# Splitting a convolution's gating by channel halves and moving the rotary products from VectorE to GpSimd

## The chip, the cores and the metric

The kernel runs on one core of a Trainium2 chip. The time is the device time of one launch in microseconds: 1805.58 us before the change, the median of three runs (1804.87 to 1806.22).

## What is computed

A decoder trunk of two layers over 256 tokens of width 1024, all in float32. Each layer has a token mixer with four branches that read one input projection, and a channel mixer (a dense SwiGLU in layer 0, eight experts in layer 1). The change touches two branches:

```
h = rms_norm(x); u = h @ w_in                 # split by columns
# C: convolution module, 512 channels
a, gt = split(u_conv); y = a * sigmoid(gt)
y = causal_depthwise_conv(y, dw, width 31) + db
y_c = silu(layer_norm(y))
# B: attention with an indexer
q, k   = rope_partial(q), rope_partial(k)     # 8 + 2 heads of 64, 16 dims rotated
qi, ki = rope_partial(qi), rope_partial(ki)   # 8 + 1 heads of 32, 8 dims rotated
rope_partial: [x1*cos - x2*sin, x2*cos + x1*sin, rest]
```

The other two branches are a pooling mixer and a state-space scan. The four are gated, summed, projected and added to x.

## The kernel before

**Weights.** All weights come in panels of 128 partitions x 2048 columns, by two DMAs each on SP's queue. A float32 product is done in three passes over a high and a low part: ScalarE copies a panel to `hi_ring` (L538), VectorE writes the remainder raw - hi to `lo_ring` (L1472), and TensorE multiplies (L964, 48 matmuls of 256 columns to a full panel). Both rings have three slots, so ScalarE can copy panel p only when TensorE is done with panel p-3. In the mixer a chunk is one or two panels and ends in a PSUM tile, `pair0` or `pair1` in turn, which ScalarE or VectorE evicts before the next chunk but one may begin. Chunks come in a fixed order: `a` (the values of the convolution), `gt` (its gates), `kwdt`, `kvqi`, `q`, `pool`, `xbc0`, `xbc1`, `z`, `g2h0` and so on.

**Order.** Each engine's program is written out by hand and synchronised by counting semaphores. On VectorE `lo_upto(n)` issues the splits up to panel n, and stands between the other work of the mixer. ScalarE's `evac` (L599) evicts a chunk.

**Convolution.** Tensor `arena` holds the values at A_P and the gates behind them. When both chunks are evicted VectorE multiplies them (L1545, 1024 columns) into a padded tile. The convolution is 31 taps x 4 channel groups of 128: the first tap is L1554, the rest are scalar_tensor_tensor instructions of 256 columns (L1557), all on VectorE, four accumulation chains in turn, with one split after every nine. TensorE then sums the channels for the layer norm (L1069).

**Rotary step.** `swap_pairs` on GpSimd's queue waits until the product has read A_P (`conved` at 1) and until q and then the indexer's keys are evicted, and copies the rotated halves, exchanged, into A_P by 6 + 12 small DMAs (L452). VectorE then does r*sin, v*cos and their sum for the indexer (3 x 256 columns) and for queries and keys (5 x 256): L1574, L1575, L1576, six instructions a layer. TensorE waits for `roped` before it swaps the keys (L1083). Later VectorE uses A_P as scratch for the pooling mixer. In layer 1 the expert stage copies a column of places on GpSimd (L485, L493) ahead of indirect DMAs.

Of the kernel before, what the change touches and what calls it, by code (L numbers as in the profile page):

```python
# [13 lines left out]

# [7 lines left out]
T = 256  # L22
# [3 lines left out]
MG = MIX // 128  # L26
# [3 lines left out]
CONV_W = 31  # L30
# [32 lines left out]
CHUNKS = [("a", 2, "A"), ("gt", 2, "A"), ("kwdt", 1, "A"), ("kvqi", 2, "A"), ("q", 2, "A"), ("pool", 2, "A"),  # L63
# [53 lines left out]
def build(nc, x_d, gains_d, consts_d, params_d, w_in, w_br, w_out, fg, fu, fd, mg, mu, md, out_d, rows_d, sum_d, cums_d):  # L117
# [3 lines left out]
    with ctx:  # L121
# [46 lines left out]
        def raw(slot):  # L168
            if slot < MRING:
# [17 lines left out]
                 "masked", "glued", "conved", "ln_summed", "centred", "ln_squared", "ln_varied", "ln_rooted",  # L187
# [75 lines left out]
        def _(sp):  # L263
# [11 lines left out]
            def mixer(L):  # L275
# [29 lines left out]
                for c0, width in ((C_A, 512), (C_GT, 512), (C_KIWI, KWDT), (C_KVQI, 512), (C_Q, 512), (C_POOL, 512),  # L305
                                  (C_XBC0, 512), (C_XBC1, 256), (C_Z, 512)):
                    if c0 == C_KIWI:
                        narrow()
                    else:
                        chunk_in(c0, width)  # L310
# [129 lines left out]
        def _(pool):  # L440
            pool.dma_start(consts[:, 0:128], consts_d[:, 0:128]).then_inc(ident_in, 16)

            def swap_pairs(L):
                pool.wait_ge(S["conved"], 4 * CONV_W * L + 1)
                pool.wait_ge(*ev(L, "q"))
                for dim, o, p, n in ((64, A_QK, A_P + 3 * T, 5 * T), (32, A_IDX, A_P, 3 * T)):
# [3 lines left out]
                    for a in range(0, 128, dim):  # L450
                        for to, fro, rows in ((a, a + half, half), (a + half, a, half), (a + 2 * half, a + 2 * half, dim - 2 * half)):
                            pool.dma_start(arena[to:to + rows, p:p + n], arena[fro:fro + rows, o:o + n]).then_inc(swapped, 16)  # L452

# [8 lines left out]
            for n in range(5):  # L462
# [7 lines left out]
                if n in (1, 3):  # L470
                    swap_pairs(n // 2)
                    spread_sums(n // 2)
# [52 lines left out]
        def _(act):  # L525
# [56 lines left out]
            def mixer(L):  # L582
# [31 lines left out]
                after("a")  # L614
                evac(ar(A_P, 1024), pair_of("a")[:, :], last=True)
                after("gt")
                evac(ar(A_P + 1024, 1024), pair_of("gt")[:, :], ACT.Sigmoid, last=True)
# [339 lines left out]
        def _(pe):  # L957
# [37 lines left out]
            def mixer(L):  # L995
# [20 lines left out]
                def t_panel(name, kh, groups=4, width=512):  # L1016
# [3 lines left out]
                    if name == "a":  # L1020
# [12 lines left out]
                t_chunk("a")  # L1033
                t_chunk("gt")
# [426 lines left out]
        def _(dve):  # L1461
# [51 lines left out]
            def mixer(L, add_dense=None):  # L1513
# [28 lines left out]
                lo_upto(6)  # L1542

                dve.wait_ge(*ev(L, "gt"))
                link(nc.vector.tensor_tensor(ypad[:, :, CPAD:], ar3(A_P, 4, T), ar3(A_P + 1024, 4, T), ALU.mult))  # L1545
                c0 = 4 * CONV_W * L
                mi = lambda o, n=16: ar(A_MISC + o, n)
                for t in range(CONV_W):
                    for g in range(MG):
                        i = t * MG + g  # L1550
                        src = ypad[:, g, t:t + T]
                        dst = ar(A_CACC + g * T, T)
                        if t == 0:
# [5 lines left out]
                        if i == 100:  # L1559
                            dve.wait_ge(S["ki_copied"], L + 1)  # L1560
                            link(nc.vector.tensor_tensor(ar3(A_MISC + 16, 2, 8), ar3(A_MISC + 16, 2, 8),
                                                         W("dt_bias", 0, 8).unsqueeze(1).broadcast_to([128, 2, 8]), ALU.add))
                            nc.vector.scalar_tensor_tensor(mi(48), mi(16), -1.0, mi(16), ALU.mult, ALU.max)\
                              .then_inc(S["dt_abs"], 1)
                        if i == 116:
                            dve.wait_ge(S["dt_exp"], L + 1)
                            nc.vector.tensor_scalar(mi(64), mi(48), 1.0, None, ALU.add).then_inc(S["dt_plus"], 1)
# [36 lines left out]
                if L == 0:  # L1604
                    dve.wait_ge(const_in, 16)
# [15 lines left out]
                s1, s2 = ar3(A_P, 4, PPAD + T), ar3(A_P + 4 * (PPAD + T), 4, PPAD + T)  # L1621
                link(nc.vector.memset(ar(A_P, 8 * (PPAD + T)).rearrange("p (g t) -> p g t", t=PPAD + T)[:, :, 0:PPAD], 0.0))
# [610 lines left out]
```

## Time and profile before

| | |
|---|---|
| median of 3 runs | 1805.58 us |
| profiled execution | 1806.82 us, span 1805.0 us, mean granted clock 0.992 |
| PE, DVE, ACT, POOL busy | 97%, 82%, 63%, 5% of the span |
| PE in the chain that ended last | 75% |
| DVE in it | 21% |

Times in the rows are microseconds from the start of the span. PE is TensorE, DVE VectorE, ACT ScalarE, POOL GpSimd; L964 is line 964 of the kernel. The chain is followed back from the last instruction, at each step to what released it. A busy time of PE says that matmuls were under way, not that it ran at its peak. The mixer of layer 0 takes about the first 315 us, that of layer 1 begins near 500 us, with the same order of work 497.4 us later.

### The profile page before, as it was taken

To read this page: it belongs to the slowest core of one execution; us is meant where nothing else is said; L and a number is where in the kernel's file an instruction comes from. 1 tells how busy PE (TensorE), PEld (TensorE's weight loads), DVE (VectorE), ACT (ScalarE), POOL (GpSimd) and SP (SyncE) were. 2 spreads that over 40 slices of the span, in tenths; PEclk is the share of its full clock that TensorE was granted. 3 is DMA by queue.
4 is the path that set the end of the run, shared out by engine and by line. 5 is a ranking of instruction groups with operands and counts; after the bars stand their busy time and mean duration, and the time that the engine had idled before them with its cause. 6 is when DMAs were issued, how large, how long until landed. Compare 5 with 4: busy or idle time off the path is not lost.

```text
span 1805.0 us, 27468 instructions
## 1 busy us (share of the span) xinstructions
PE 1752.9 (97%) x10329; PEld 1535.4 (85%) x10329; DVE 1485.7 (82%) x1483; ACT 1144.2 (63%) x976; POOL 84.4 (5%) x101
## 2 busy tenths in 40 slices
PE   7999999999999999999999999999999999999997
PEld 6988888999989988887888888888888888888886
DVE  4998976544459989768979889888898898988987
ACT  4356664444353566646757777777777777777775
POOL 0200000000002000000010000000000000000000
PEclk9999999999999999999999999999999999999999
DMA  8554545755345545448989999999999999999994
GB/s 273 165 163 150 168 150 173 245 187 185 117 153 166 166 142 165 162 173 308 365 320 364 402 365 386 391 375 387 376 365 399 366 387 385 368 397 370 376 407 158
DMA packets 239922, 501.68 MB, mean 278 GB/s; under 512 B 20512, under 2 KB 45104, under 8 KB 239712
## 3 DMA queue, kind: packets, MB, share of 16 engines
q1 hardware_dynamic: 233552, 480.18, 73.9%
q0 software_dynamic: 6288, 20.38, 3.8%
q8 instruction: 55, 0.90, 0.2%
q14 instruction: 27, 0.22, 0.0%
HBM read 490.52 MB, written 7.88 MB: 276 GB/s over the span
## 4 chain that ended last, share of the span: by engine, by line
PE 75%; DVE 21%; ACT 2%; issue 1%; DMA 0%; SPq 0%; DVEq 0%; ACTq 0%
PE pair L964 51%; PE aux L964 20%; DVE lo_ring L1472 7%; DVE arena L1557 5%; PE pair L1387 1%; ACT hi_ring L538 1%; DVE arena L1697 1%; DVE arena L1683 1%; DVE small L1696 1%; DMA raw_ring<-in_w_in 0%; DVE arena L1657 0%; PE aux L1364 0%; DVE act_lo L1647 0%; PE aux L1357 0%; DVE arena L1628 0%
## 5 line engine op out<-in xcount | busy, mean ns | idle before, releaser
L1472 DVE TENSOR_TENSOR lo_ring<-raw_ring,hi_ring 128x2048 fp32r<-128x2048 f32 x276 | 623.5, 2262 | 129.0 <-ACT hi_ring L538 127.1
L538 ACT ACTIVATE hi_ring<-raw_ring 128x2048 fp32r<-128x2048 f32 x276 | 522.4, 1894 | 250.0 <-PE pair L964 170.3
L1472 DVE TENSOR_TENSOR lo_ring<-arena,hi_ring 128x2048 fp32r<-128x2048 f32 x183 | 418.3, 2289 | 75.6 <-ACT hi_ring L538 75.6
L538 ACT ACTIVATE hi_ring<-arena 128x2048 fp32r<-128x2048 f32 x183 | 350.4, 1919 | 138.3 <-PE pair L964 73.0
L964 PE MATMUL pair<-hT_lo,hi_ring 128*128 128x256 f32 (+1 forms) x1360 | 389.9, 287 | 12.9 <-DVE lo_ring L1472 7.0
L964 PE MATMUL pair<-hT_hi,lo_ring 128*128 128x256 f32 (+1 forms) x1360 | 385.8, 284 | 0.0
L964 PE MATMUL pair<-hT_hi,hi_ring 128*128 128x256 f32 (+1 forms) x1360 | 385.7, 284 | 0.0
L964 PE MATMUL pair<-lo_ring,hT_hi 128*128 128x512 f32 x896 | 354.5, 396 | 0.1
L964 PE MATMUL pair<-hi_ring,hT_hi 128*128 128x512 f32 x896 | 349.6, 390 | 0.0
L964 PE MATMUL pair<-hi_ring,hT_lo 128*128 128x512 f32 x896 | 348.8, 389 | 0.0
L964 PEld LDWEIGHTS pair<-hT_lo,hi_ring 128*128 128x128 f32 (+1 forms) x1360 | 260.9, 192 | 21.9 <-issue 8.0
L964 PEld LDWEIGHTS pair<-hT_hi,lo_ring 128*128 128x128 f32 (+1 forms) x1360 | 261.0, 192 | 0.4
L964 PEld LDWEIGHTS pair<-hT_hi,hi_ring 128*128 128x128 f32 (+1 forms) x1360 | 260.9, 192 | 0.0
L964 PEld LDWEIGHTS pair<-hi_ring,hT_hi 128*128 128x128 f32 x896 | 168.2, 188 | 36.2
L964 PEld LDWEIGHTS pair<-lo_ring,hT_hi 128*128 128x128 f32 x896 | 168.3, 188 | 34.2 <-DVE hT_lo L2119 0.5
L964 PEld LDWEIGHTS pair<-hi_ring,hT_lo 128*128 128x128 f32 x896 | 168.5, 188 | 33.4
L964 PE MATMUL aux<-lo_ring,hid_hi 128*128 128x512 f32 x448 | 176.3, 394 | 0.8 <-DVE lo_ring L1472 0.6
L964 PE MATMUL aux<-hi_ring,hid_hi 128*128 128x512 f32 x448 | 175.1, 391 | 0.0
L964 PE MATMUL aux<-hi_ring,hid_lo 128*128 128x512 f32 x448 | 175.1, 391 | 0.0
L964 PEld LDWEIGHTS aux<-lo_ring,hid_hi 128*128 128x128 f32 x448 | 84.6, 189 | 19.7 <-issue 1.7
L964 PEld LDWEIGHTS aux<-hi_ring,hid_hi 128*128 128x128 f32 x448 | 84.5, 189 | 17.8
L964 PEld LDWEIGHTS aux<-hi_ring,hid_lo 128*128 128x128 f32 x448 | 84.5, 189 | 17.1
(319 smaller groups left out, 1789.9 us busy)
## 6 DMA issues: line engine op xcount, KB each, us to landing
raw_ring<-in_mu SPq DMA_DIRECT2D x222, 512.0 KB, 5.9
arena<-in_mg SPq DMA_DIRECT2D x220, 512.0 KB, 5.6
raw_ring<-in_w_in SPq DMA_DIRECT2D x120, 512.0 KB, 4.5
arena<-in_md SPq DMA_DIRECT2D x114, 512.0 KB, 5.5
raw_ring<-in_md SPq DMA_DIRECT2D x110, 512.0 KB, 5.7
raw_ring<-in_w_br SPq DMA_DIRECT2D x32, 512.0 KB, 4.6
raw_ring<-in_w_out SPq DMA_DIRECT2D x16, 512.0 KB, 4.5
raw_ring<-in_fg SPq DMA_DIRECT2D x12, 512.0 KB, 4.0
```

The costliest lines, as they stand in the source:

```text
L538: nc.scalar.activation(hi_ring[:, h, 0:cols], raw(slot)[:, 0:cols], ACT.Copy).then_inc(hi_ready, 1)
L964: ins = pe.matmul(out, l, r, start=first and n == 0, stop=last and n == 2, skip_group_check=True)
L1387: ins = pe.transpose(pairs[1][:, k * 128:(k + 1) * 128], ar(A_HID + k * 128, 128), C("ident"))
L1472: nc.vector.tensor_tensor(lo_ring[:, h, 0:cols], raw(slot)[:, 0:cols], hi_ring[:, h, 0:cols].bitcast(f32), ALU.subtract).then_inc(lo_ready, 1)
L1557: ins = nc.vector.scalar_tensor_tensor(dst, src, W("conv_dw", g * CONV_W + t), dst, ALU.mult, ALU.add)
L1683: ins = nc.vector.scalar_tensor_tensor(sc, ar(A_P + h * w, w), ar(A_MISC + 8 * b + h, 1), consts[:, far - w:far] if h == 0 else sc, ALU.mu ...
L1696: link(nc.vector.max(best, sc))
L1697: link(nc.vector.match_replace(sc, best, sc, TAKEN))
```

## The change

The input chunks `a` and `gt` become `glu0` and `glu1`: each holds two of the four channel groups, values in the first 512 columns and gates in the second. Their panels are filled by one DMA of 4 x 256 columns for the values and one for the gates. ScalarE evicts each chunk in two instructions, a copy and a sigmoid. VectorE multiplies a half as soon as its chunk is evicted, and runs the convolution over the 31 taps of the first half and then of the second; the second product is issued after 24 convolution instructions. A split now stands after every eight, and four instead of six stand ahead of it all.

The six rotary instructions leave VectorE and are issued by GpSimd behind its swap DMAs, with a semaphore (`turning`) of their own. The swap waits for the 25th convolution instruction, and VectorE waits for `roped` only before it reuses A_P for pooling.

```diff
-CHUNKS = [("a", 2, "A"), ("gt", 2, "A"), ("kwdt", 1, "A"), ("kvqi", 2, "A"), ("q", 2, "A"), ("pool", 2, "A"),
+CHUNKS = [("glu0", 2, "A"), ("glu1", 2, "A"), ("kwdt", 1, "A"), ("kvqi", 2, "A"), ("q", 2, "A"), ("pool", 2, "A"),
...
-                for c0, width in ((C_A, 512), (C_GT, 512), (C_KIWI, KWDT), (C_KVQI, 512), (C_Q, 512), (C_POOL, 512),
+                def glu_in(half):
+
+                    nonlocal i
+                    for kh in range(2):
+                        slot, _ = MSLOT[L][i]
+                        if slot in last:
+                            sp.wait_ge(lo_ready, last[slot] + 1)
+                        v = raw(slot).rearrange("p (k n) -> p k n", n=512)
+                        for q, c0 in enumerate((C_A, C_GT)):
+                            sp.dma_start(v[:, :, q * 256:(q + 1) * 256],
+                                         w_in[L, kh * 512:(kh + 1) * 512, c0 + half * 256:c0 + (half + 1) * 256]
+                                         .rearrange("(k p) n -> p k n", p=128)).then_inc(raw_in[slot], 16)
+                        last[slot] = MIX_BASE[L] + i
+                        i += 1
+
+                glu_in(0)
+                glu_in(1)
...
-                pool.wait_ge(S["conved"], 4 * CONV_W * L + 1)
+                pool.wait_ge(S["conved"], 4 * CONV_W * L + 25)
...
+            def rope(L, o, n, p, cs, sn, last):
+                v, r = ar3(o, n, T), ar3(p, n, T)
+                for c, t in ((sn, r), (cs, v)):
+                    nc.gpsimd.tensor_tensor(t, t, C(c).unsqueeze(1).broadcast_to([128, n, T]), ALU.mult).then_inc(S["turning"], 1)
+                pool.wait_ge(S["turning"], 4 * L + (4 if last else 2))
+                ins = nc.gpsimd.tensor_tensor(v, v, r, ALU.add)
+                if last:
+                    ins.then_inc(S["roped"], 1)
...
+                    if n == 1:
+                        pool.wait_ge(const_in, 16)
+                    pool.wait_ge(swapped, 16 * 18 * (n // 2 + 1))
+                    rope(n // 2, A_IDX, 3, A_P, "cosi", "sini", False)
+                    rope(n // 2, A_QK, 5, A_P + 3 * T, "cosq", "sinq", True)
...
-                after("a")
-                evac(ar(A_P, 1024), pair_of("a")[:, :], last=True)
-                after("gt")
-                evac(ar(A_P + 1024, 1024), pair_of("gt")[:, :], ACT.Sigmoid, last=True)
+                for half in range(2):
+                    name = f"glu{half}"
+                    after(name)
+                    evac(ar(A_P + half * 512, 512), pair_of(name)[:, 0:512])
+                    evac(ar(A_P + 1024 + half * 512, 512), pair_of(name)[:, 512:1024], ACT.Sigmoid, last=True)
...
-                lo_upto(6)
-
-                dve.wait_ge(*ev(L, "gt"))
-                link(nc.vector.tensor_tensor(ypad[:, :, CPAD:], ar3(A_P, 4, T), ar3(A_P + 1024, 4, T), ALU.mult))
+                lo_upto(4)
+
                 c0 = 4 * CONV_W * L
                 mi = lambda o, n=16: ar(A_MISC + o, n)
-                for t in range(CONV_W):
-                    for g in range(MG):
-                        i = t * MG + g
-                        src = ypad[:, g, t:t + T]
-                        dst = ar(A_CACC + g * T, T)
-                        if t == 0:
-                            ins = nc.vector.tensor_scalar(dst, src, W("conv_dw", g * CONV_W), W("conv_b", g), ALU.mult, ALU.add)
-                        else:
-                            dve.wait_ge(S["conved"], c0 + i - MG + 1)
-                            ins = nc.vector.scalar_tensor_tensor(dst, src, W("conv_dw", g * CONV_W + t), dst, ALU.mult, ALU.add)
-                        ins.then_inc(S["conved"], 1)
...
-                        if i % 9 == 8:
-                            lo_upto(min(done[0] + 1, CH_PANEL["g2h0"] + 1))
-
-                def rope(o, n, p, cs, sn):
-                    v = ar3(o, n, T)
-                    r = ar3(p, n, T)
-                    link(nc.vector.tensor_tensor(r, r, C(sn).unsqueeze(1).broadcast_to([128, n, T]), ALU.mult))
-                    link(nc.vector.tensor_tensor(v, v, C(cs).unsqueeze(1).broadcast_to([128, n, T]), ALU.mult))
-                    return nc.vector.tensor_tensor(v, v, r, ALU.add)
+
+                def glu(half):
+                    dve.wait_ge(*ev(L, f"glu{half}"))
+                    o = half * 512
+                    link(nc.vector.tensor_tensor(ypad[:, 2 * half:2 * half + 2, CPAD:], ar3(A_P + o, 2, T), ar3(A_P + 1024 + o, 2, T),
+                                                 ALU.mult))
+
+                glu(0)
+
+                for i, (half, t, q) in enumerate(product(range(2), range(CONV_W), range(2))):
+                    g = 2 * half + q
+                    if i == 24:
+                        glu(1)
+                    src = ypad[:, g, t:t + T]
+                    dst = ar(A_CACC + g * T, T)
+                    if t == 0:
+                        ins = nc.vector.tensor_scalar(dst, src, W("conv_dw", g * CONV_W), W("conv_b", g), ALU.mult, ALU.add)
+                    else:
+                        dve.wait_ge(S["conved"], c0 + i - 1)
+                        ins = nc.vector.scalar_tensor_tensor(dst, src, W("conv_dw", g * CONV_W + t), dst, ALU.mult, ALU.add)
+                    ins.then_inc(S["conved"], 1)
...
+                    if i % 8 == 7:
+                        lo_upto(min(done[0] + 1, CH_PANEL["g2h0"] + 1))
...
-                dve.wait_ge(swapped, 16 * 18 * (L + 1))
-                link(rope(A_IDX, 3, A_P, "cosi", "sini"))
                 lo_upto(CH_PANEL["g2h1"] + 1)
-                rope(A_QK, 5, A_P + 3 * T, "cosq", "sinq").then_inc(S["roped"], 1)
-                dve.wait_ge(S["roped"], L + 1)
...
+                dve.wait_ge(S["roped"], L + 1)
+                if L == 0:
+                    dve.wait_ge(const_in, 16)
```

The start of the convolution on VectorE, layer 0, in the kernel before (arena holds activations, L1472 is a split, L1545 the product, L1554 and L1557 the convolution):

```order
L1472 TENSOR_TENSOR lo_ring<-raw_ring,hi_ring 128x2048 x3
L1472 TENSOR_TENSOR lo_ring<-raw_ring,hi_ring 128x384
L1472 TENSOR_TENSOR lo_ring<-raw_ring,hi_ring 128x2048
L1545 TENSOR_TENSOR arena<-arena 128x4x256
L1554 TENSOR_SCALAR arena<-arena,params 128x256 x4
L1557 SCALAR_TENSOR_TENSOR arena<-arena,params 128x256 x5
L1472 TENSOR_TENSOR lo_ring<-raw_ring,hi_ring 128x2048
L1557 SCALAR_TENSOR_TENSOR arena<-arena,params 128x256 x9
```

The same place in the changed kernel (L1505 is the split, L1583 the product, L1595 and L1598 the convolution):

```order
L1505 TENSOR_TENSOR lo_ring<-raw_ring,hi_ring 128x2048 x3
L1583 TENSOR_TENSOR arena<-arena 128x2x256
L1595 TENSOR_SCALAR arena<-arena,params 128x256 x2
L1598 SCALAR_TENSOR_TENSOR arena<-arena,params 128x256 x6
L1505 TENSOR_TENSOR lo_ring<-raw_ring,hi_ring 128x384
L1598 SCALAR_TENSOR_TENSOR arena<-arena,params 128x256 x8
L1505 TENSOR_TENSOR lo_ring<-raw_ring,hi_ring 128x2048
L1598 SCALAR_TENSOR_TENSOR arena<-arena,params 128x256 x8
L1505 TENSOR_TENSOR lo_ring<-raw_ring,hi_ring 128x2048
L1583 TENSOR_TENSOR arena<-arena 128x2x256
L1598 SCALAR_TENSOR_TENSOR arena<-arena,params 128x256 x8
```

Two splits moved from ahead of the product to behind it, and the product is in two parts.

GpSimd's queue in layer 0 in the kernel before, from the last swap DMAs on (L456 and L460 are the spreading of running sums for the state-space scan):

```order
L452 DMA arena<-arena 4x768 x2
L452 DMA arena<-arena 24x768
L456 DMA cums<-arena 8x256
L460 DMA arena<-cums 128x256 x8
```

And in the changed kernel (L470 is the swap, L475 and L477 the rotary products and sums, L483 and L487 the spreading):

```order
L470 DMA arena<-arena 4x768 x2
L470 DMA arena<-arena 24x768
L475 ISA
L475 TENSOR_TENSOR arena<-arena,consts 128x768 x2
L477 TENSOR_TENSOR arena<-arena 128x768
L475 TENSOR_TENSOR arena<-arena,consts 128x1280 x2
L477 TENSOR_TENSOR arena<-arena 128x1280
L483 DMA cums<-arena 8x256
L487 DMA arena<-cums 128x256 x8
```

The six tensor operations stand between the swap and the spreading DMAs; on VectorE they are gone.

## Rows read from the trace of the kernel before

**Rows 1.** The page's part 4: shares of the chain that ended last, by engine.
```profile
PE 75%; DVE 21%; ACT 2%; issue 1%; DMA 0%; SPq 0%; DVEq 0%; ACTq 0%
```

**Rows 2.** The chain in order of time, layer 0: start us, us, what.
```profile
66.80 3.56 DVE arena L1557 x9
70.36 2.20 DVE lo_ring L1472
...
172.33 0.50 DVE arena L1683
```

**Rows 3.** Busy time by stretch, VectorE: stretch, us, busy, clock, DMA share, GB/s.
```profile
42.00:202.00 160.00, 153.03 (x282) 1.00 0.51 161
```

**Rows 4.** TensorE's waits, 42 to 202 us; last row: 540 to 700 us, where it differs.
```profile
PE pair L964 <- DVE lo_ring L1472: 3.5, 3, 2.0
PE aux L1137 <- DVE arena L1736: 1.5, 1, 1.5
PE pair L964 <- issue: 1.0, 1, 1.0
PE pair L964 <- DVE arena L1657: 0.5, 1, 0.5
PE pair L1069 <- DVE arena L1557: 0.4, 1, 0.4
...
PE pair L964 <- DVE arena L1657: 0.4, 1, 0.4
```

**Rows 5.** VectorE in order of time: start, us, instruction, [idle before <-releaser].
```profile
37.86 2.29 DVE L1472 TENSOR_TENSOR lo_ring<-raw_ring,hi_ring 128x2048 fp32r<-128x2048 f32 x1 [5.74 <-ACT hi_ring L538]
42.67 1.23 DVE L1545 TENSOR_TENSOR arena<-arena 128x1024 f32<-128x1024 f32 x1 [2.52 <-ACT arena L599]
```

**Rows 6.** ScalarE in order of time, layer 0.
```profile
30.09 1.02 ACT L599 ACTIVATE arena<-pair 128x1024 f32<-128x1024 f32 x1 [3.46 <-PE pair L964]
...
37.85 1.28 ACT L599 ACT_TABLE_LOAD   x1
...
92.60 3.97 ACT L538 ACTIVATE hi_ring<-raw_ring 128x2048 fp32r<-128x2048 f32 x2
97.44 0.60 ACT L599 ACTIVATE arena<-pair 128x512 f32<-128x512 f32 x1 [0.86 <-PE pair L964]
```

**Rows 7.** TensorE in order of time, layer 0.
```profile
99.41 0.36 PE L964 MATMUL pair<-hT_lo,hi_ring 128*128 128x256 f32 x1 [2.01 <-DVE lo_ring L1472]
...
134.20 0.60 PE L1083 MATMUL aux<-arena,consts 128*128 128x256 f32 x2
```

**Rows 8.** VectorE in order of time: first and last of six rotary instructions.
```profile
122.96 0.95 DVE L1574 TENSOR_TENSOR arena<-arena,consts 128x768 f32<-128x768 f32 x1
...
131.19 1.49 DVE L1576 TENSOR_TENSOR arena<-arena 128x1280 f32<-128x1280 f32 x1
```

**Rows 9.** GpSimd in order of time; then a DMA issue: KB each, us to landing.
```profile
81.27 6.04 POOL L452 DMA_DIRECT2D arena<-arena  x12 [9.13 <-ACT arena L634]
...
arena<-arena POOLq DMA_DIRECT2D x16, 12.0 KB, 2.9
```

**Rows 10.** VectorE and GpSimd side by side, expert stage of layer 1.
```profile
915.09 2.29 DVE L1472 TENSOR_TENSOR lo_ring<-arena,hi_ring 128x2048 fp32r<-128x2048 f32 x1
915.21 2.22 POOL L485 COPY place_in<-place 128x1 uint32<-128x1 uint32 x1 [96.61 <-DVE arena L2091]
...
932.10 2.29 DVE L1472 TENSOR_TENSOR lo_ring<-arena,hi_ring 128x2048 fp32r<-128x2048 f32 x1 [0.43 <-ACT hi_ring L538]
933.72 0.72 POOL L485 COPY place_in<-place 128x1 uint32<-128x1 uint32 x1 [14.38 <-PE aux L1364]
```

**Rows 11.** The chain, two panels; then busy time, all engines, granted clock (PEclk) near the end.
```profile
223.73 5.94 PE pair L964 x48
...
236.00 8.54 PE pair L964 x48
...
227.00:245.00 18.00, 16.02 (x119) 14.77 (x119) 11.01 (x21) 13.34 (x14) 0.00 (x0) 0.81 0.37 120
```

More of the change, by code:

```diff
@@ L15 @@
+from itertools import product
 import numpy as np
@@ L186, in build @@
                  "ki_turned", "ki_copied", "roped", "k_swapped", "k_copied", "indexed", "relued", "scored",
-                 "masked", "glued", "conved", "ln_summed", "centred", "ln_squared", "ln_varied", "ln_rooted",
+                 "masked", "glued", "conved", "turning", "ln_summed", "centred", "ln_squared", "ln_varied", "ln_rooted",
                  "ln_scaled", "pooled", "pool_mixed", "branch_f", "branch_hi", "branch_lo", "merged_done",
@@ L303, in narrow @@
                     i += 1
-                for c0, width in ((C_A, 512), (C_GT, 512), (C_KIWI, KWDT), (C_KVQI, 512), (C_Q, 512), (C_POOL, 512),
+                def glu_in(half):
[13 more added lines that the diff above has]
+                glu_in(1)
+                for c0, width in ((C_KIWI, KWDT), (C_KVQI, 512), (C_Q, 512), (C_POOL, 512),
                                   (C_XBC0, 512), (C_XBC1, 256), (C_Z, 512)):
@@ L1019, in t_panel @@
                         free(name)
-                    if name == "a":
+                    if name == "glu0":
                         pe.wait_ge(S["hT_lo_done"], 8 * L + 2 * kh + 2)
@@ L1031, in t_chunk @@
                         t_panel(name, kh, groups, width)
-                t_chunk("a")
-                t_chunk("gt")
+                t_chunk("glu0")
+                t_chunk("glu1")
                 free("kwdt")
@@ L1541, in mixer @@
                 dve.wait_ge(param_in, 16 * (L + 1))
-                lo_upto(6)
-                dve.wait_ge(*ev(L, "gt"))
-                link(nc.vector.tensor_tensor(ypad[:, :, CPAD:], ar3(A_P, 4, T), ar3(A_P + 1024, 4, T), ALU.mult))
+                lo_upto(4)
                 c0 = 4 * CONV_W * L
                 mi = lambda o, n=16: ar(A_MISC + o, n)
-                for t in range(CONV_W):
-                    for g in range(MG):
-                        i = t * MG + g
-                        src = ypad[:, g, t:t + T]
-                        dst = ar(A_CACC + g * T, T)
-                        if t == 0:
-                            ins = nc.vector.tensor_scalar(dst, src, W("conv_dw", g * CONV_W), W("conv_b", g), ALU.mult, ALU.add)
-                        else:
-                            dve.wait_ge(S["conved"], c0 + i - MG + 1)
-                            ins = nc.vector.scalar_tensor_tensor(dst, src, W("conv_dw", g * CONV_W + t), dst, ALU.mult, ALU.add)
-                        ins.then_inc(S["conved"], 1)
[L1559 to L1567, printed above, removed]
-                        if i % 9 == 8:
-                            lo_upto(min(done[0] + 1, CH_PANEL["g2h0"] + 1))
@@ new lines, in mixer @@
+                glu(0)
[11 more added lines that the diff above has]
+                    ins.then_inc(S["conved"], 1)
+                    if i == 100:
+                        dve.wait_ge(S["ki_copied"], L + 1)
+                        link(nc.vector.tensor_tensor(ar3(A_MISC + 16, 2, 8), ar3(A_MISC + 16, 2, 8),
+                                                     W("dt_bias", 0, 8).unsqueeze(1).broadcast_to([128, 2, 8]), ALU.add))
+                        nc.vector.scalar_tensor_tensor(mi(48), mi(16), -1.0, mi(16), ALU.mult, ALU.max)\
+                          .then_inc(S["dt_abs"], 1)
+                    if i == 116:
+                        dve.wait_ge(S["dt_exp"], L + 1)
+                        nc.vector.tensor_scalar(mi(64), mi(48), 1.0, None, ALU.add).then_inc(S["dt_plus"], 1)
+                    if i % 8 == 7:
+                        lo_upto(min(done[0] + 1, CH_PANEL["g2h0"] + 1))
@@ L1603, in mixer @@
                 ins.then_inc(S["centred"], 1)
-                if L == 0:
-                    dve.wait_ge(const_in, 16)
-                dve.wait_ge(swapped, 16 * 18 * (L + 1))
-                link(rope(A_IDX, 3, A_P, "cosi", "sini"))
                 lo_upto(CH_PANEL["g2h1"] + 1)
-                rope(A_QK, 5, A_P + 3 * T, "cosq", "sinq").then_inc(S["roped"], 1)
-                dve.wait_ge(S["roped"], L + 1)
                 dve.wait_ge(S["ln_varied"], L + 1)
```

## The prediction, made before the changed kernel ran

> **What bounds the kernel now.** I read the chain of waits first. TensorE (PE) holds three quarters of it and VectorE (DVE) 21% [rows 1], so most of the program is bound by the matmuls and the change can act only where VectorE is in the chain. That is one stretch per layer, about 42 to 202 us and again 497.4 us later: nine convolution instructions in 3.56 us, then one split of a weight panel ("lo") in 2.20 us, over and over [rows 2]. VectorE is busy 153.0 of those 160 us [rows 3]. The period of 5.76 us is also nearly what TensorE needs for a panel (5.94 us for 48 matmuls [rows 11]), so the two are almost balanced. The list of TensorE's waits tells how much a faster VectorE could give there: 3.5 + 1.5 + 1.0 + 0.5 + 0.4 = 6.9 us in layer 0; in layer 1 the 0.4 is missing and the last one is 0.4, so 6.4 us [rows 4]. Whatever VectorE saves beyond this buys nothing. The largest wait, 2.0 us, ends at 99.41, when the split of the first z panel arrives [rows 7]: TensorE had finished at 97.4.
>
> **Part 1: halves of channels.** Before, the product value x gate waits for all four panels and starts at 42.67; VectorE stood idle 5.74 us and 2.52 us just ahead of it [rows 5]. After, TensorE finishes half 0 (values and gates) when it used to finish the values: their eviction starts at 30.09. Two half evictions of 0.60 us and a table load of 1.28 us [rows 6] put the product at about 32.5. It costs two products of half size, some 0.1 us more. The convolution chain of one channel group now returns after two instructions, not four. A piece of this size that waits for its predecessor takes 0.50 us in the chain [rows 2], so two interleaved chains need 0.25 us per instruction, less than the 0.40 us that one takes: no cost. The split now comes after eight instructions (8 x 0.395 + 2.20 = 5.36 us), a little faster than TensorE. Panel DMAs have the same bytes in rows half as long; I take 0 and allow 0.5 us either way for the very first, which is in the chain.
>
> Where is VectorE when the swap lands? From 32.5: two products 1.4, 88 convolution instructions 34.8, the short split 0.5, eight full splits 17.6, two half ones 2.3: 89.1 us, with eight more instructions and then the split of the z panel. Undisturbed it would do these by 92.3, wait for ScalarE's copy (first of the two of rows 6 at 92.60, ready at about 94.6) and deliver at 96.8, ahead of TensorE's 97.4. All of the 2.0 us would go, and the convolution would end at about 113.
>
> **Part 2: rotary on GpSimd.** VectorE loses three instructions of 0.95 us and three of 1.49 us, 7.3 us per layer [rows 8]. GpSimd (POOL) gets them behind its DMAs. Its twelve late ones run from 81.27 to 87.3, and a small one lands 2.9 us after issue [rows 9], so the work starts at about 90.0. The scratch area, which the swap overwrites, is free when the second product is done, at about 48.3 us, before GpSimd issues anything; the new count costs nothing. Behind it in GpSimd's queue stand the spreading of the running sums and later loads, which wait for work beyond the convolution anyway. TensorE reads the rotated keys at 134.2 [rows 7], so GpSimd has over 40 us. Taken alone it is free.
>
> It is not alone. GpSimd's one-column copy of 915.21 took 2.22 us and ended at 917.43; VectorE's subtraction of two SBUF operands had run 915.09 to 917.38. The one of 933.72 ended at 934.44, that subtraction at 934.39 [rows 10]. GpSimd waited out the whole VectorE instruction, twice to within 0.05 us. Nearly all that VectorE does from 90 us on (convolution and splits) is of this kind, and the moved operations read two operands each. No row shows VectorE held by GpSimd, since before GpSimd never ran anything long. If the path is exclusive it must work in this direction too. The Trainium skill, "SBUF — State Buffer", section "Who interferes with whom", says that it is: a VectorE instruction with two SBUF inputs and a GpSimd one that reads SBUF exclude each other for the whole instruction. By that rule, the trace agrees in the one direction that it shows.
>
> How long does GpSimd hold it? Lower end 0 (no holding). Next, VectorE's own time, 7.3 us. From 0.95 us at 768 columns and 1.49 us at 1280, VectorE pays 1.055 ns per column and 0.14 us fixed. I take it that GpSimd has only the shared path and fetches two operands through it one after the other: twice the column part, 2 x 6.48, plus 6 x 0.14 = 13.8 us, which I use. Upper end twice that, 27.6 us, since no row has a GpSimd operation of size. The Trainium skill, "GPSIMD Engine Reference", section "3.1 Elementwise — side-by-side cycle accounting", gives 4497 ns for 2048 columns of such an operation; its estimate for 6144 columns is 13.5 us and would make the sum 0.6 us smaller. No run here shows it.
>
> **The sum.** At 90.0 VectorE has six instructions (2.4) and the split (2.2) to go; with 13.8 of holding it delivers at 108.4. TensorE waits 11.0 us at 97.4 instead of 2.0: +9.0. From there TensorE needs three panels, 17.5 us, to the sum over channels, near 126; VectorE ends the convolution near 124.5 (113 + 11.6) and is then 7.3 us lighter, so it stays ahead of TensorE and the other waits go: 4.9 us in layer 0, 4.4 in layer 1. Layer 0 is +4.1, layer 1 +4.6. Then the clock: after a stretch of small work and a 1.4 us wait, 48 matmuls took 8.54 us against 5.94, at a granted clock of 0.81 over that window [rows 11]. Eleven idle microseconds may bring the same drop to the lower level, 0 to 2.6 us per layer; I take half, 1.3, twice 2.6. Total +11.3 us. Against the profiled execution's own 1806.8 (span 1805.0 and 1.8 around it) that is 1818.1; that execution is 1.2 us over the median of 1805.6, so the forecast is 1816.9, rounded to 1817. Slower, because the wait only moves: its place (the z panel) is the same, its cause is GpSimd.
>
> **Rivals.** (a) VectorE isn't held. For it: no row shows it held. Against it: rows 10. Then all waits go, 6.9 + 6.4 = 13.3 us: 1792.3. (b) It is held for about 7.3 us only (GpSimd as fast as VectorE, or holding in part). The split is at 101.9, TensorE waits 4.5 instead of 2.0; per layer +2.5 - 4.9 and +2.5 - 4.4, together -4.3: 1801.3, with a clock drop up to 1803.9. The head start then pays for the holding. TensorE's wait grows by the holding less 4.8 us and the others save 4.65 on the mean, so the break-even is 9.4 us of holding without a clock drop, 8.1 with 1.3 us of it. (c) GpSimd needs 27.6 us: per layer 13.8 more, 1844.5. Against it: its one-column copies take about as long as VectorE's small ones when free, so its fixed cost is small. (d) The head start fails, because the split or ScalarE's copies are late after the new order, or GpSimd is late for TensorE's 134.2: little speaks for it, over 25 us of slack.
>
> **How the numbers follow.** Holding of the size I take: 0.64, with 1810 to 1824 as its own range (holding 11.5 us without clock cost: +4.1; 16 us with 2.6 per layer: +18.3). (a) 0.15, (b) 0.13, (c) 0.05, (d) or something unseen 0.03. The range goes from 1799, which takes in (b), to 1826; left out are (a) and (c), 0.20. A change of 0.2%, 3.6 us, is about what can be told from none here. Faster by more: (a), most of (b) and a bit: 0.24. Within: the rest of (b) and half of (d): 0.10. Slower: 0.66.
>
> **What would show it.** In the new profile the six GpSimd operations should stand from about 90 us on, the larger ones at about 2.8 us without waiting; in the same stretch VectorE's convolution instructions of 0.47 us should show some of 2 to 3 us, or idle time as long, and TensorE should wait some 11 us for a split at about 97 and again at 595. VectorE's first product should start at 32 to 33. After 135 us TensorE's waits on VectorE should be nearly gone. Convolution instructions of 0.47 us throughout with GpSimd running beside them would prove me wrong, as would a wait at 97 under 5 us; a wait of over 20 us would be (c).

## The result and the profile after the change

The changed kernel takes 1812.47 us, the median of six runs (1812.33 to 1812.91), against 1805.61 us for the kernel before on the same chip (six runs). The ratio is 1.0037, with a 95% interval of 1.0025 to 1.005: 6.9 us slower. The profiled execution took 1812.91 us with a span of 1811.1 us, 6.1 us more than before, at a mean granted clock of 0.989 (0.992).

First the page's part 4, the shares of the chain that ended last:

```profile
PE 82%; DVE 13%; ACT 3%; issue 1%; DMA 1%; SPq 0%; DVEq 0%; ACTq 0%
```

VectorE fell from 21% to 13% [rows 1]. By that line alone the change looks like a success: VectorE was relieved. But the time is longer. VectorE's share fell because TensorE, once it has waited long for VectorE, hardly waits for it again in the mixer, and the chain stays on TensorE.

The head start of part 1, on VectorE in order of time (start, us, instruction, idle time before it and its releaser):

```profile
32.94 0.69 DVE L1583 TENSOR_TENSOR arena<-arena 128x512 f32<-128x512 f32 x1 [2.82 <-ACT arena L631]
...
89.32 3.25 DVE L1598 SCALAR_TENSOR_TENSOR arena<-arena,params 128x256 f32<-128x256 f32 x8
94.85 3.54 DVE L1505 TENSOR_TENSOR lo_ring<-raw_ring,hi_ring 128x2048 fp32r<-128x2048 f32 x1 [2.29 <-ACT hi_ring L570]
98.32 11.63 DVE L1598 SCALAR_TENSOR_TENSOR arena<-arena,params 128x256 f32<-128x256 f32 x5
...
111.35 2.28 DVE L1505 TENSOR_TENSOR lo_ring<-raw_ring,hi_ring 128x2048 fp32r<-128x2048 f32 x1
```

The product starts at 32.94 where it started at 42.67 [rows 5]. Eight convolution instructions take 3.25 us. Then five of them take 11.63 us, and the split ahead of them 3.54 instead of 2.29. Beside that, GpSimd:

```profile
92.57 3.67 POOL L475 TENSOR_TENSOR arena<-arena,consts 128x768 f32<-128x768 f32 x2 [4.92 <-DMA arena<-arena]
96.32 3.78 POOL L477 TENSOR_TENSOR arena<-arena 128x768 f32<-128x768 f32 x1
100.06 6.19 POOL L475 TENSOR_TENSOR arena<-arena,consts 128x1280 f32<-128x1280 f32 x2
106.33 2.94 POOL L477 TENSOR_TENSOR arena<-arena 128x1280 f32<-128x1280 f32 x1
```

The six rotary operations run from 92.57 to 109.27. Taken one by one, four of the five convolution instructions are long, and each ends some 0.3 us behind one operation of GpSimd: 2.06 us against the one of 768 columns, 3.10 to 3.18 us against those of 1280. The fifth takes 0.47 us, when GpSimd is done. Two of each engine:

```profile
100.06 3.15 POOL L475 TENSOR_TENSOR arena<-arena,consts 128x1280 f32<-128x1280 f32 x1
100.31 3.18 DVE L1598 SCALAR_TENSOR_TENSOR arena<-arena,params 128x256 f32<-128x256 f32 x1
103.17 3.08 POOL L475 TENSOR_TENSOR arena<-arena,consts 128x1280 f32<-128x1280 f32 x1
103.41 3.13 DVE L1598 SCALAR_TENSOR_TENSOR arena<-arena,params 128x256 f32<-128x256 f32 x1
```

What TensorE makes of it is in its waits, 42 to 202 us (us in total, times, longest):

```profile
PE pair L997 <- DVE lo_ring L1505: 10.0, 2, 9.2
PE pair L997 <- issue: 0.2, 1, 0.2
```

The waits of 1.5, 1.0 and 0.5 us [rows 4] are gone or nearly so, the one of 0.4 stands just behind the stretch, at 206 us, and a single wait of 9.2 us has come. The chain of waits shows how it is made up:

```profile
92.92 1.91 ACT hi_ring L570
94.83 0.02 issue
94.85 3.54 DVE lo_ring L1505
98.40 11.55 DVE arena L1598 x5
...
111.43 2.21 DVE lo_ring L1505
113.64 0.04 issue
113.69 14.20 PE pair L997 x96
```

TensorE waits for the split at 111.43, which stands behind the five slow convolution instructions. Then 96 matmuls take 14.20 us, where two panels of 48 at the full rate take 11.9 us. The clock says why (PE, PEld, DVE, ACT and POOL busy, then the granted clock, DMA share, GB/s):

```profile
113.00:120.00 7.00, 6.31 (x32) 6.31 (x33) 7.00 (x13) 0.70 (x1) 0.00 (x0) 0.55 0.45 152
```

A granted clock of 0.55 is nearly all at the lower level (1.2 of 2.4 GHz). TensorE had idled for 9.2 us just before.

### The profile page after: what moved, and what is told of

It is laid out like the page before. It is cut to its first block, busy times and chain, and to the rows that moved or that the text cites. A ratio compares the mean times of both kernels' runs of the same rounds, so it can differ in the third digit from the quotient of the medians.

```text
span 1811.1 us, 27475 instructions
## 1 busy us (share of the span) xinstructions
PE 1751.1 (97%) x10329; PEld 1534.2 (85%) x10329; DVE 1493.0 (82%) x1473; ACT 1144.9 (63%) x980; POOL 117.8 (7%) x113
## 4 chain that ended last, share of the span: by engine, by line
PE 82%; DVE 13%; ACT 3%; issue 1%; DMA 1%; SPq 0%; DVEq 0%; ACTq 0%
PE pair L997 58%; PE aux L997 20%; DVE lo_ring L1505 4%; DVE arena L1598 1%; PE pair L1420 1%; ACT hi_ring L570 1%; DVE arena L1728 1%; DVE arena L1714 1%; DVE small L1727 1%; DMA raw_ring<-in_w_in 1%; DVE arena L1688 0%; PE aux L1397 0%; DVE arena L1659 0%; PE aux L1390 0%; DVE act_lo L1678 0%
## 5 line engine op out<-in xcount | busy, mean ns | idle before, releaser
L1505 DVE TENSOR_TENSOR lo_ring<-raw_ring,hi_ring 128x2048 fp32r<-128x2048 f32 x276 | 625.7, 2270 | 118.3 <-ACT hi_ring L570 116.7
L1505 DVE TENSOR_TENSOR lo_ring<-arena,hi_ring 128x2048 fp32r<-128x2048 f32 x183 | 418.2, 2289 | 76.5 <-ACT hi_ring L570 76.4
L1598 DVE SCALAR_TENSOR_TENSOR arena<-arena,params 128x256 f32<-128x256 f32 x240 | 117.0, 557 | 0.1
```

Of the source, the lines that this page charges most:

```text
L1505: nc.vector.tensor_tensor(lo_ring[:, h, 0:cols], raw(slot)[:, 0:cols], hi_ring[:, h, 0:cols].bitcast(f32), ALU.subtract).then_inc(lo_ready, 1)
```

## Experiments

No kernel here leaves out any of the computation; those with idle work add operations whose results nobody reads.

My theory: GpSimd's operations on two SBUF operands lock VectorE out for as long as they last, in turns. The rivals: GpSimd's queue or its DMAs disturb the split by themselves, or the new order of the convolution costs what it should have gained. The first four runs take the change apart.

**Part 1 alone (e1).** The changed kernel with the rotary step back on VectorE:

```diff
-                    rope(n // 2, A_IDX, 3, A_P, "cosi", "sini", False)
-                    rope(n // 2, A_QK, 5, A_P + 3 * T, "cosq", "sinq", True)
...
+                link(rope(A_IDX, 3, A_P, "cosi", "sini"))
+                rope(A_QK, 5, A_P + 3 * T, "cosq", "sinq").then_inc(S["roped"], 1)
```

> Halves of channels as in the change, the six rotary instructions back on VectorE at their old place. Theory (GpSimd holding VectorE makes the whole loss, the head start is a gain): VectorE ends the convolution about 4.5 us earlier, the 2.0 us wait at the z panel goes and most of the later ones too, about 4 to 5 us per layer, so 1796 to 1798 us, with no VectorE instruction of 128x256 above 0.5 us. Rival (the new order of halves, the half-length DMA rows or the shorter accumulation chains cost the time, and GpSimd is harmless): 1806 to 1812 us.

Measured: 1794.95 us (1793.33 to 1796.29), ratio 0.9943 [0.993, 0.9957]. The halves alone gain 10.6 us. On VectorE the place that took 11.63 us, and TensorE's waits in 42 to 202 us:

```profile
95.18 2.29 DVE L1491 TENSOR_TENSOR lo_ring<-raw_ring,hi_ring 128x2048 fp32r<-128x2048 f32 x1 [2.29 <-ACT hi_ring L556]
97.39 2.06 DVE L1584 SCALAR_TENSOR_TENSOR arena<-arena,params 128x256 f32<-128x256 f32 x5
```

```profile
PE aux L1156 <- DVE arena L1763: 1.5, 1, 1.5
PE pair L983 <- issue: 1.0, 1, 1.0
PE pair L983 <- DVE lo_ring L1491: 0.7, 1, 0.7
PE pair L983 <- DVE arena L1684: 0.4, 1, 0.4
```

Five instructions take 2.06 us, and the waits for splits are 0.7 us in all, down from 3.5 [rows 4]. The order of part 1 costs nothing that it should gain; that rival falls.

The time is below the expected 1796 to 1798 us. Where it was gained can be read without the list of waits: all these kernels run the same 10329 matmuls in the same order (e9 has 72 more), so the starts of the same matmul in two traces can be compared, and where the distance between them changes, time is won or lost. Against the profiled kernel before, e1 starts 0.6 us late, gains 4.8 us between 94.6 and 188.3 us (layer 0) and 5.0 us in the same stretch of layer 1, as expected (4 to 5), and 2.8 us outside them (1.1 between 188 and 248 us, 1.7 behind 686 us), where the kernel before has more matmuls at the lower clock. I had not counted those.

**Part 2 alone (e2).** The old chunks and order, with the rotary step on GpSimd as in the change:

```diff
+                    rope(n // 2, A_IDX, 3, A_P, "cosi", "sini", False)
+                    rope(n // 2, A_QK, 5, A_P + 3 * T, "cosq", "sinq", True)
...
-                link(rope(A_IDX, 3, A_P, "cosi", "sini"))
...
-                rope(A_QK, 5, A_P + 3 * T, "cosq", "sinq").then_inc(S["roped"], 1)
```

> The old order of the convolution (one product, four chains), with the six rotary instructions moved to GpSimd as in the change. Theory: VectorE has no idle time when GpSimd starts, so it is held for the full 13 to 14 us per layer; TensorE's waits around the z panels grow from 2.0 to about 14 us, the later ones go; +8 to +10 us per layer, 1822 to 1828 us. Rival (GpSimd is harmless): VectorE is 7.3 us lighter per layer after the convolution, 1799 to 1803 us.

Measured: 1822.73 us (1820.21 to 1823.89), ratio 1.0092 [1.0078, 1.0106]: 17 us slower. VectorE, then TensorE's waits:

```profile
94.42 16.28 DVE L1571 SCALAR_TENSOR_TENSOR arena<-arena,params 128x256 f32<-128x256 f32 x9
110.63 2.28 DVE L1486 TENSOR_TENSOR lo_ring<-raw_ring,hi_ring 128x2048 fp32r<-128x2048 f32 x1
```

```profile
PE pair L978 <- DVE lo_ring L1486: 14.6, 1, 14.6
PE pair L978 <- issue: 0.2, 1, 0.2
```

Nine instructions take 16.28 us instead of 3.65, 12.6 us held. The two parts simply add up: part 1 gives -10.6 and part 2 alone +17.2, which makes +6.6, and the change is +6.9.

**Idle reads (e3).** Part 1, and on GpSimd behind the swap six products of the same sizes on an area that is not yet in use. VectorE still does the rotary step. The edit also has VectorE clear that area at the start of each layer, and ScalarE wait for the products late in the mixer.

```diff
+            def idle_work(L):
+                for k, m in enumerate((768, 768, 768, 1280, 1280, 1280)):
+                    ins = nc.gpsimd.tensor_tensor(ar(A_GATES, m), ar(A_GATES, m), ar(A_GATES + 768, m), ALU.mult)
+                    ins.then_inc(S["turning"], 1)
+                    pool.wait_ge(S["turning"], 6 * L + k + 1)
```

> As the kernel with halves alone, rotary on VectorE, and in addition six GpSimd multiplications (3 x 768 and 3 x 1280 columns, two SBUF inputs) on an area that nobody uses at that time, behind the same swap DMAs; their result is thrown away. Theory: VectorE is held for 11 to 14 us per layer with no relief, 12 to 16 us per two layers above the changed kernel's saving, so 1819 to 1826 us; VectorE's convolution instructions show durations of 2 to 3 us. Rival (GpSimd doesn't hold VectorE): within 0.1% of the kernel with halves alone.

Measured: 1823.15 us (1822.78 to 1823.26), ratio 1.0099 [1.0084, 1.0114], 28 us over e1. GpSimd, then VectorE:

```profile
93.39 16.80 POOL L474 TENSOR_TENSOR arena<-arena 128x768 f32<-128x768 f32 x6 [5.04 <-DMA arena<-arena]
```

```profile
99.24 11.63 DVE L1594 SCALAR_TENSOR_TENSOR arena<-arena,params 128x256 f32<-128x256 f32 x5
```

Of the 28 us, 24 arise in the two held stretches (12.1 and 11.8 us, by the starts of the same matmuls). Another 2.3 us come near 525 us, where the clearing (1.76 us on VectorE) stands in front of layer 1's first weight panel and TensorE waits 2.0 us; that is the experiment's own cost and not GpSimd's. On VectorE it is the same 11.63 us, from operations on which no one depends but a late wait of ScalarE. It is the running of the operations that costs, not any dependence on them.

**Idle writes (e4).** As e3, with memsets, which read nothing:

```diff
-                    ins = nc.gpsimd.tensor_tensor(ar(A_GATES, m), ar(A_GATES, m), ar(A_GATES + 768, m), ALU.mult)
+                    ins = nc.gpsimd.memset(ar(A_GATES + 1024, m) if m <= 1024 else ar(A_GATES, m), 0.0)
```

Here VectorE needn't clear the area.

> As the one before, but the six GpSimd operations are memsets of the same sizes: they write SBUF and read nothing. Theory (what is shared is the read path): equal to the kernel with halves alone, 1796 to 1798 us, no long VectorE instruction. Rival (GpSimd at work holds VectorE whatever it does): each memset holds it for its duration, some 6 to 8 us per layer, 1803 to 1812 us.

Measured: 1796.06 us (1795.42 to 1796.37), ratio 0.9948 [0.9932, 0.9963], as e1. The intervals overlap. GpSimd, then VectorE:

```profile
93.75 6.04 POOL L474 MEMSET arena<- 128x768 f32 x6 [5.11 <-DMA arena<-arena]
```

```profile
98.08 2.06 DVE L1593 SCALAR_TENSOR_TENSOR arena<-arena,params 128x256 f32<-128x256 f32 x5
```

GpSimd operations beside VectorE that write only do not hold it at all: one of 1280 columns ran from 96.15 to 97.33 us, wholly inside the split of 95.87, and the split took its 2.29 us. This separates the theory from its rival: the queue, the swap DMAs and the semaphores are those of e3.

**Idle copies (e7).** As e3, with one operand:

```diff
-                    ins = nc.gpsimd.tensor_tensor(ar(A_GATES, m), ar(A_GATES, m), ar(A_GATES + 768, m), ALU.mult)
+                    ins = nc.gpsimd.tensor_copy(ar(A_GATES, m), ar(A_GATES + 768, m))
```

> As the kernel with idle GpSimd multiplications, but each is a copy with one SBUF input, same sizes, result thrown away. Theory (GpSimd reads through the shared path and holds it for the whole instruction, one input or two): six copies of together 6 to 7 us, VectorE held for 4 to 5 us per layer, 1801 to 1805 us, with VectorE instructions of 1 to 1.8 us among the convolution. Rival (only two-input GpSimd operations hold): 1794 to 1796 us.

Measured: 1806.61 us (1805.69 to 1807.53, ten runs), ratio 1.0004 [0.9994, 1.0013]. GpSimd, then VectorE:

```profile
93.56 8.81 POOL L474 COPY arena<-arena 128x768 f32<-128x768 f32 x6 [5.56 <-DMA arena<-arena]
```

```profile
97.43 5.62 DVE L1594 SCALAR_TENSOR_TENSOR arena<-arena,params 128x256 f32<-128x256 f32 x5
```

A GpSimd operation with a single SBUF operand holds VectorE too, 5.62 - 2.06 = 3.6 us. The time is 11.7 us over e1, more than expected (1801 to 1805 us). Between the profiled executions it is 12.8 us. By the starts of the same matmuls, 6.1 of them come with the two waits for the held splits and 2.9 with slow-clock matmuls right behind them. Another 2.3 come near 515 us, where e7, like e3, clears its area on VectorE, and 1.6 near 912 us with more slow-clock matmuls than e1 has. I foresaw none of these but the waits, and only the first two belong to the hold.

**How much of the step can move (e5, e6).** e5 moves only the first product to GpSimd, so that it fits in VectorE's own wait for ScalarE; e6 moves the indexer's three operations.

```diff
+            def turn_part(L):
+                r = ar3(A_P, 3, T)
+                nc.gpsimd.tensor_tensor(r, r, C("sini").unsqueeze(1).broadcast_to([128, 3, T]), ALU.mult).then_inc(S["turning"], 1)
```

> Halves of channels, and of the six rotary instructions only the first (indexer halves times sine, 768 columns) on GpSimd; five stay on VectorE. Theory (what counts is whether VectorE wants the path at that time): the operation takes 1.84 us and starts at about 92.5, inside the 2.3 us in which VectorE waits for ScalarE's copy, so it holds nothing, and VectorE loses 0.95 us per layer: 1793 to 1795 us against 1795.0 for halves alone. Rival (every GpSimd operation costs VectorE its own duration): 1796 to 1798 us.

```diff
+                for c, t in (("sini", r), ("cosi", v)):
+                    nc.gpsimd.tensor_tensor(t, t, C(c).unsqueeze(1).broadcast_to([128, 3, T]), ALU.mult).then_inc(S["turning"], 1)
+                pool.wait_ge(S["turning"], 3 * L + 2)
+                nc.gpsimd.tensor_tensor(v, v, r, ALU.add).then_inc(S["turning"], 1)
```

> Halves of channels, the indexer's three rotary instructions (3 x 768 columns) on GpSimd, the three of queries and keys on VectorE. Theory: GpSimd works 5.5 us per layer, of which 2.3 fall into VectorE's wait, so VectorE is held 3.2 us and is 2.9 us lighter: about even, 1794 to 1798 us. Rival (the loss comes with any work on GpSimd, in proportion to its columns: 17.5 us for 6144, so 6.6 us for 2304): 1800 to 1803 us.

Measured: e5 1794.29 us (1792.4 to 1794.38), ratio 0.9933 [0.9919, 0.9946]; e6 1795.3 us (1793.42 to 1796.54), ratio 0.994 [0.9927, 0.9954]. Neither can be told from e1. In e6 the price is there and is paid back, VectorE and then TensorE's waits:

```profile
96.98 5.25 DVE L1595 SCALAR_TENSOR_TENSOR arena<-arena,params 128x256 f32<-128x256 f32 x5
```

```profile
PE pair L994 <- DVE lo_ring L1502: 2.8, 1, 2.8
```

VectorE is held 3.2 us in these five and 0.2 us in the split ahead of them, and TensorE waits 2.8 us for the split instead of 0.7, while the wait of 1.5 us vanishes, since VectorE has 2.9 us less to do (three operations of 0.95 us [rows 8]). e1, e5 and e6 are the fastest versions of this study.

**Smaller pieces (e8).** The changed kernel with each rotary operation cut into pieces of 256 columns, 24 per layer:

```diff
-                    nc.gpsimd.tensor_tensor(t, t, C(c).unsqueeze(1).broadcast_to([128, n, T]), ALU.mult).then_inc(S["turning"], 1)
+                    for j in range(n):
+                        nc.gpsimd.tensor_tensor(t[:, j, :], t[:, j, :], C(c), ALU.mult).then_inc(S["turning"], 1)
```

> The changed kernel with each of GpSimd's six operations cut into pieces of 256 columns, 24 per layer. Theory (the path is held instruction by instruction, and the two engines take turns): the longest VectorE instruction of the convolution falls from 3.5 to about 1.1 us, VectorE finishes some 24 instead of 6 instructions beside GpSimd, and since the time held is the same plus the pieces' fixed cost the kernel takes 1811 to 1816 us. Rival (GpSimd keeps the path until its queue is empty, or VectorE gets it first whenever it asks): durations as in the changed kernel, or a GpSimd stretch well over 30 us with TensorE waiting at most 3 us for the split.

Measured: 1809.43 us (1808.15 to 1810.19, ten runs), ratio 1.002 [1.0011, 1.0029], 3 us better than the whole change and below the expected 1811 to 1816 us. On VectorE:

```profile
94.86 2.92 DVE L1509 TENSOR_TENSOR lo_ring<-raw_ring,hi_ring 128x2048 fp32r<-128x2048 f32 x1 [2.28 <-ACT hi_ring L574]
97.70 4.47 DVE L1602 SCALAR_TENSOR_TENSOR arena<-arena,params 128x256 f32<-128x256 f32 x5
102.10 0.71 DVE L1606 TENSOR_TENSOR arena<-arena,params 128x16 f32<-128x16 f32 x1
```

A convolution instruction takes some 0.95 us where it took 2.1 to 3.2: the turns are one instruction each, and a shorter one on GpSimd holds for less. VectorE's instructions from 94.86 to 118.65 took 10.4 us more than they take when free, about as much as in the whole change (10.8), but spread over more panels: three waits for splits of 7.3 us in all, the longest 5.0.

**A warm wait (e9).** The changed kernel, with 36 throwaway matmuls on TensorE between the two z panels, where it waits:

```diff
-                t_chunk("z")
+                t_panel("z", 0)
+                pe.wait_ge(*ev(L, "xbc1"))
+                pe.wait_ge(S["ident_done"], 1)
+                for _ in range(36):
+                    pe.matmul(pairs[1][:, 0:512], ident_r[:, :],
+                              ident_r[:, :].unsqueeze(1).broadcast_to([128, 4, 128]), start=True, stop=True)
+                t_panel("z", 1)
```

> The changed kernel with 36 matmuls of 512 columns on scratch (about 8.1 us) between the two z panels, where TensorE waits 9.2 us for the split; the split and all else as in the changed kernel. Theory (part of the loss is the clock's drop after that wait: the 96 matmuls behind it took 14.20 and 13.64 us where 11.77 is usual): they take 11.8 us again, 2.4 and 1.9 us less, so 1807.5 to 1810 us against 1812.5. Rival (the drop has another cause, or is made up for by other drops later): 1811 to 1814 us, with the same granted clock of 0.97 in the stretch 42 to 202 us.

Measured: 1809.49 us (1808.0 to 1811.23, eleven runs), ratio 1.0022 [1.0013, 1.0031], 3.0 us less than the change (2.6 with each set against its own runs of the kernel before). The chain, then the stretches of the two layers, in both of which the change had a clock of 0.97:

```profile
98.89 11.69 DVE arena L1604 x5
...
114.33 11.77 PE pair L997 x96
```

```profile
42.00:202.00 160.00, 157.44 (x1261) 150.69 (x1259) 148.36 (x256) 85.64 (x101) 26.39 (x25) 1.00 0.51 159
540.00:700.00 160.00, 157.97 (x1265) 151.23 (x1263) 148.37 (x257) 85.57 (x101) 26.77 (x25) 1.00 0.50 159
```

The hold is unchanged, the 96 matmuls take 11.77 us instead of 14.20 (in layer 1 11.77 instead of 13.64), and the clock is 1.00. The slow clock behind the wait is thus a consequence of the idling. Directly it costs 2.4 and 1.9 us; the medians give back 3.0 in all, since drops elsewhere change too (the profiled execution has a longer one near 912 us).

**After the convolution (e10).** The change, with GpSimd's rotary step waiting for the convolution's last instruction:

```diff
+                    pool.wait_ge(S["conved"], 4 * CONV_W * (n // 2 + 1))
```

> The changed kernel with GpSimd's six operations held back until VectorE has finished the convolution (about 113 us in layer 0). Theory (the holding costs what VectorE would do at that time on the shared path; there it has about 2 us of waiting for TensorE's sum, and TensorE isn't short of a split until later): TensorE's 10 us wait at the z panels disappears, smaller ones come between 117 and 140 us, 4 to 6 us per layer over halves alone, 1802 to 1808 us. Rival (the loss is the same wherever the operations stand): 1811 to 1814 us; a third way, rotated keys late for TensorE's swap, would show as a wait of TensorE on GpSimd near 132 us.

Measured: 1814.36 us (1812.49 to 1814.57), ratio 1.0048 [1.0034, 1.0062]. The expectation (1802 to 1808 us) missed. The wait for the z panel is gone, but TensorE now waits for the layer norm, first row below; the cause is on VectorE, the rows after it:

```profile
PE pair L1109 <- ACT arena L710: 9.7, 1, 9.7
```

```profile
115.19 1.82 DVE L1616 TENSOR_SCALAR arena<-arena 128x16 f32<-128x16 f32 x1
117.04 1.78 DVE L1618 TENSOR_SCALAR arena<-arena 128x16 f32<-128x16 f32 x1
118.85 0.18 DVE L1619 TENSOR_TENSOR arena<-arena 128x16 f32<-128x16 f32 x1
118.94 1.83 DVE L1620 TENSOR_TENSOR arena<-arena 128x16 f32<-128x16 f32 x1
...
121.09 2.56 DVE L1622 TENSOR_TENSOR arena<-arena 128x16 f32<-128x16 f32 x1
123.69 2.80 DVE L1623 TENSOR_TENSOR arena<-arena 128x16 f32<-128x16 f32 x1
```

Such 16-column instructions take 0.16 to 0.18 us when free. Here six of them (five in the rows, one more behind them) wait for GpSimd, 1.6 to 2.6 us each. I had priced the hold by how much work VectorE has there; what counts is how many instructions stand in front of what is needed, since each can lose a turn.

## Why the prediction was right

It said 1817 us and slower; measured 1812.5, in the likeliest case's own range of 1810 to 1824. Against the profiled execution the sum was +11.3 us, and +6.1 came. The direction and the cause were right. The sum was 5.2 us too high, 3.4 of them in the two stretches that it was about and 1.8 outside them, and one of my own signs of being wrong came up.

**Part 1: right.** Product at 32.5, measured 32.94; eviction at 30.09, measured 30.41, TensorE's first weight panel having come 0.3 us later. Eight instructions in 3.25 us, so two interleaved chains are indeed enough. e1 shows the part's worth when nothing else changes.

**GpSimd's own time: right.** Predicted 13.8 us. Free of waiting, the 768-column operation takes 1.85 us (half of the 3.67 us pair in the rows above, the first two running largely in VectorE's idle time) and the 1280-column one 2.94: 3 x 1.85 + 3 x 2.94 = 14.4 us. The Trainium skill, "GPSIMD Engine Reference", section "3.1 Elementwise — side-by-side cycle accounting", states 4497 ns for 2048 columns of such an operation, from which 13.5 us is an estimate for these; the runs are some 7% above it.

**The hold: right in kind and size.** e2, e3 and the change show it, e4 and e1 its absence. VectorE lost 3.54 - 2.28 = 1.3 us in the split and 11.63 - 2.06 = 9.6 us in five instructions, 10.8 us. The sum had it 11.6 us late: of the 13.8 us of holding, 2.2 fell into VectorE's own wait for ScalarE's copy. In the sum's way of counting the measured hold is thus some 13.0 us. GpSimd started at 92.57 and not at 90.0. I took 2.9 us from issue to landing, the figure for transfers of 12 KB; the last one of the swap has 72 KB (24 rows of 768 values; such ones took 4.3 us to land here, the median of four), and GpSimd idled 4.92 us behind its issue. The direction that the kernel before could not show agrees with the Trainium skill, "SBUF — State Buffer", section "Who interferes with whom": both engines wait out the other's instruction, for its whole length.

**Where TensorE waits: one panel off.** I put the whole wait at the first z panel, at 97.4 us, as if all of the hold stood ahead of its split. But the engines take turns, and GpSimd began late: that split lost one turn, 1.3 us, and TensorE waited 0.8 us. "A wait at 97 under 5 us" was to prove me wrong, and it came. What it was a sign for, a VectorE that isn't held, is refuted by the five instructions behind that split: the wait came one panel on, 9.2 us at 104.5.

By the starts of the same matmuls in both traces, the stretches from the first z panel to 188.3 us and the same one of layer 1 changed so (us, sums of the parts rounded):

| | predicted, layer 0 and 1 | layer 0 | layer 1 |
|---|---|---|---|
| waits for the z panels | +9.0, +9.0 | +8.1 | +8.0 |
| clock | +1.3, +1.3 | +2.4 | +0.6 |
| TensorE's other waits | -4.9, -4.4 | -6.1 | -5.1 |
| together | +5.4, +5.9 | +4.4 | +3.5 |

**The other waits: worth more than listed.** They went, as predicted. But I took them from the list of waits, which shows short ones too short: with the one of 0.60 us at 135.39 in the kernel before, 0.97 us pass between two matmuls between which 0.03 pass in the change. So the premise that a faster VectorE can give 6.9 and 6.4 us and nothing beyond was wrong, and so was the price of rival (a): in the two stretches e1 gained 9.8 us (1.3 of it clock), though its listed waits are only 6.3 us shorter.

**The clock: right in kind, incomplete.** I added 1.3 us per layer. Behind the long waits it cost 2.4 us (14.20 us for 96 matmuls instead of 11.77) and 1.9. But the kernel before lost to slow clocks as well, and I left those out. In layer 1 it has a slow stretch of its own near 597 us, worth 1.3 us, which is gone. Between 188 and 248 us the change is 1.1 us faster: the panel that took 8.54 us [rows 11] runs at the full rate, which is 2.6 us less, but TensorE then idles for work of ScalarE and VectorE. And the layer norm between the two layers was 1.0 us shorter at a higher clock:

```profile
508.00:519.00 11.00, 9.13 (x48) 6.86 (x47) 10.34 (x22) 6.96 (x17) 0.54 (x1) 1.00 0.66 195
```

(In the kernel before the clock there was 0.84.) I priced the new drop and forgot that the old ones are not fixed.

The two mixers (+4.4 and +3.5), the start (+0.3), the panel at 236 us (-1.1), the layer norm (-1.0) and the rest (-0.1) make +6.1, rounded. Why the clock drops in one of two orders of the same work and not in the other is not shown, apart from the drop behind the long wait (e9).

**The rivals.** (a), VectorE not held, fell with e2 and e3. (b), held 7.3 us, and (c), 27.6 us, fell with the measured hold, 13.0 us as they count it. My break-even of 8.1 to 9.4 us of holding agrees with the change (13.0, slower than before) and with e6 (3.4 us late, 5.6 counted so, faster); no run stands near enough to it to show where it is.

## What to carry to other kernels

Before moving work from a bounding engine to an idle one, look for what both share: here VectorE got rid of 7.3 us and lost 10.8, because GpSimd's operations that read SBUF and VectorE's took turns, one instruction each. What is hurt is the first thing needed that stands behind several instructions of VectorE while GpSimd runs, however small they are. Take the parts of such a change apart: one of the two here was worth 10.6 us.

## What the runs showed of the hardware

- GpSimd and VectorE take turns by instruction. A convolution instruction of 0.41 us takes 2.1 us against a GpSimd product or sum of 768 columns and 3.1 to 3.2 us against one of 1280 (the change, e3); against one of 256 columns some 0.95 us (e8).
- It isn't only two-operand work: one-operand copies on GpSimd hold VectorE (3.6 us with 6144 columns copied, part of them in VectorE's idle time, e7), and a 16-column VectorE instruction with one SBUF tensor was held 1.6 us (e10). Memsets on GpSimd hold nothing (e4).
- GpSimd's own times here: product or sum 1.85 us at 768 columns and 2.94 at 1280; a copy 0.83 and 1.33; a memset 0.74 and 1.18.
- A waiting GpSimd idled 4.1 to 5.7 us behind the last issue of a row of small SBUF-to-SBUF transfers, the last of 72 KB (4.13 us in e2, 5.71 in e6).
